# First operands of a recurrence made beside its decays' projections, loads in another order, squares ahead of weight sums, and products of ones on an idle TensorE

## The reference

```python
for i in range(2):                      # first block
    if i % 2 == 0:
        z = rmsnorm(h, mix_norm) @ mix_w_in          # 1024 x 3328
        y_a = rwkv7_bidir(z[..., :1792], ...)        # recurrence, both directions
        y_b = hyena_bidir(z[..., 1792:], ...)        # long convolution, filters made by a small MLP
        h = h + concat([y_a, y_b]) @ mix_w_out
    else:                                # neighbourhood attention
        ...
    h = h + conv_ffn(...); h = h + per_layer_embedding(...)

# rwkv7_bidir: r, k, v are neighbour-mixed slices of z
w  = exp(-exp(-softplus(-(w0 + tanh(wd) @ w_up)) - 0.5))   # decays
a  = sigmoid(a0 + ad @ a_up);  g = sigmoid(gd) @ g_up
kk = k * k_k / max(norm(k * k_k), 1e-12);  k = k * (1 + (a - 1) * k_a)
S  = S * w - (S kk) (kk a)^T + v k^T;  y = S r            # 256 steps

for l in range(2):                      # second block, 256 tokens and 256 of context
    x, ctx = half_ffn(...); x, ctx = token_mixing(...); x, ctx = half_ffn(...)
# half_ffn: h + 0.5 * gate * ((silu(n @ wg) * (n @ wu)) @ wd), n = modulate(rms_norm(h))
```

## Time and profile before

| | |
|---|---|
| median of 3 runs | 3163.56 us (3161.01 to 3167.01) |
| the profiled execution | 3160.99 us, its span 3159.5 us |
| mean granted TensorE clock | 0.985 |
| busy: PE, DVE, ACT, POOL | 95%, 44%, 18%, 1% |
| weights and tables read | 367.19 MB, mean 117 GB/s |

### The profile page before, as it was taken

How to read it: one execution, slowest core, us unless ns; L and a number is a source line. 1 busy time by engine, 2 the same in 40 slices (tenths; PEclk the granted TensorE clock), 3 DMA queues, 4 the chain that set the end, 5 groups by cost and what they waited for, 6 DMA issues and landing times.

```text
span 3159.5 us, 43436 instructions
## 1 busy us (share of the span) xinstructions
PE 2995.4 (95%) x18294; PEld 2415.3 (76%) x18294; DVE 1375.0 (44%) x2855; ACT 583.6 (18%) x1342; POOL 37.3 (1%) x60
## 2 busy tenths in 40 slices
PE   7978899999899989999999899999999999999999
PEld 5756678898488968888844447888878888765899
DVE  3265433533533534445222625445244453225675
ACT  1232222113312021000021621010010000224110
POOL 0000000002000000000000000000000000000000
PEclk9989999999999999999999999999999999999999
DMA  6668754356244442222212112222422322331353
GB/s 223 214 215 284 273 172 159 109 185 174 80 137 140 128 159 75 86 64 74 90 56 75 54 40 67 80 74 63 117 80 80 93 61 74 108 103 44 123 156 106
DMA packets 355844, 371.03 MB, mean 117 GB/s; under 512 B 7395, under 2 KB 282228, under 8 KB 355524
## 3 DMA queue, kind: packets, MB, share of 16 engines
q1 hardware_dynamic: 350224, 358.24, 36.0%
q0 software_dynamic: 2208, 5.31, 0.9%
q10 hardware_dynamic: 3220, 4.71, 0.4%
HBM read 367.19 MB, written 1.05 MB: 117 GB/s over the span
## 4 chain that ended last, share of the span: by engine, by line
PE 89%; DVE 6%; ACT 3%; issue 2%; DMA 1%; ACTq 0%; DVEq 0%
PE acc L132 73%; PE aux L132 15%; ACT sb_xn L267 1%; PE aux L2150 1%; DVE sb_work L1415 0%; DMA weights<-mix_w_in 0%; DVE sb_work L1886 0%; DVE sb_work L1883 0%; ACT sb_work L1685 0%; ACT sb_work L1687 0%; DMA sb_x<-xT 0%; DVE sb_work L1897 0%; ACT sb_rstd L258 0%; DVE sb_work L1665 0%; ACT sb_rstd L260 0%
## 5 line engine op out<-in xcount | busy, mean ns | idle before, releaser
L132 PE MATMUL acc<-sb_xn,weights 128*128 128x256 f32 (+2 forms) x5184 | 1220.1, 391 | 31.4 <-ACT sb_xn L267 17.6
L132 PEld LDWEIGHTS acc<-sb_xn,weights 128*128 128x128 f32 x5184 | 951.2, 192 | 257.3 <-issue 136.0
L132 PE MATMUL acc<-sb_work 128*128 128x256 f32 (+1 forms) x1936 | 373.1, 346 | 0.0
L132 PEld LDWEIGHTS acc<-sb_work 128*128 128x128 f32 x1936 | 323.0, 191 | 34.1
L132 PE MATMUL acc<-sb_work,weights 128*128 128x256 f32 (+2 forms) x1508 | 322.4, 361 | 3.2 <-DVE sb_work L1200 1.4
L132 PE MATMUL acc<-sb_big,weights 128*128 128x256 f32 (+1 forms) x1776 | 313.8, 333 | 4.1 <-issue 3.9
L132 PEld LDWEIGHTS acc<-sb_big,weights 128*128 128x128 f32 x1776 | 278.1, 191 | 30.8 <-issue 5.3
L132 PEld LDWEIGHTS acc<-sb_work,weights 128*128 128x128 f32 x1508 | 254.2, 191 | 54.3 <-issue 26.1
L1415 DVE TENSOR_TENSOR sb_work<-weights 128x512 f32<-128x512 f32 (+1 forms) x112 | 99.7, 890 | 160.5 <-PE acc L132 160.4
L1387 ACT COPY sb_work<-acc 128x256 f32<-128x256 f32 (+1 forms) x112 | 37.9, 339 | 704.2 <-PE acc L132 704.2
L132 PE MATMUL aux<-sb_xn,sb_work 128*128 128x256 f32 (+1 forms) x704 | 153.2, 362 | 6.5 <-ACT sb_xn L267 6.5
(11 more groups left out here) (304 smaller groups left out, 2553.0 us busy)
## 6 DMA issues: line engine op xcount, KB each, us to landing
weights<-ffn_w_up SPq DMA_DIRECT2D x88, 1024.0 KB, 7.9
weights<-w_mod SPq DMA_DIRECT2D x36, 2048.0 KB, 9.0
weights<-ffn_w_down SPq DMA_DIRECT2D x48, 1408.0 KB, 7.1
weights<-ffn_w_gate SPq DMA_DIRECT2D x44, 1024.0 KB, 5.5
weights<-w_in SPq DMA_DIRECT2D x8, 2048.0 KB, 8.0
weights<-mix_w_in SPq DMA_DIRECT2D x6, 2048.0 KB, 13.5
weights<-na_w_qkv SPq DMA_DIRECT2D x6, 2048.0 KB, 9.9
weights<-ple_w_gate SPq DMA_DIRECT2D x4, 2048.0 KB, 8.2
```

Source lines behind the costliest of these rows:

```text
L132: return te.matmul(o, lhsT, rhs, start=start, stop=stop, skip_group_check=True)
```

## The change

Six things are changed.

1. Loads: x is issued first on ACT's queue, then the four constants. The filter tables, the DFT matrices and the context move to SP's queue, between the blocks of `mix_w_in`. The masks' DMAs on POOL wait for x. The waits for the constants move behind the first norm's squares (DVE) and sums (PE); ACT's SiLU of the conditions moves behind the first norm.
2. PE gets products of ones with ones (`tensor_idle`), 128 x 128 each, whose result nobody reads: 22 at the program's start, 8 behind the first norm's sums, and 11 behind the sums of each of the six norms of the second block.
3. The four gate products go ahead of the projections, into two accumulator banks, and ACT copies them out with two wide copies ahead of the sigmoids.
4. For p = 0 the mixed key is made before DVE waits for the projections; ACT makes the key's copy and square between the sigmoids of n = 3 and n = 4, and PE sums the squares between n = 5 and n = 6. The temporaries get other places, and for p = 0 two of them are `dd` and `rho`. DVE's two modulation steps go behind the mixes.
5. ACT's first copy of the scan for p = 0 waits for the bonus sum.
6. In a half FFN DVE squares the odd tiles before the weight sums and scales, not behind them.

The core of the diff:

```diff
+    def tensor_idle(n):
+
+        for _ in range(n):
+            mm(aux[3][:, 0:128], ones[:], ones[:])
+
     def tensor_mix_in():
         tensor_norm(mix_norm)
+        tensor_idle(8)
+        te.wait_ge(const_in.sem, 64)
...
-    def scalar_lora(other):
+    def scalar_lora(other, first):
         ac.wait_ge(wad_set.sem, wad_set_at(1))
         wad_tanh.on(ac.activation(wad[0:64], wad[0:64], ACT.Tanh))
         other.to(14)
+        for b in range(2):
+            ac.wait_ge(gate.sem, gate_at(b))
+            gate_read.on(ac.copy(gg[:, 2 * b:2 * b + 2, :], area(acc[b], 0, 2, L)))
         for n in range(NG):
...
+            if n == 3:
+                next(first)
         other.to(MOD_EARLY)
-        for ct in range(CT):
-            ac.wait_ge(gate.sem, gate_at(ct))
-            gate_read.on(ac.copy(gg[:, ct, :], aux[ct][:, 0:L]))
...
+        for b in range(2):
+            te.wait_ge(acc_free[b].sem, scan_banks[b])
+            for ct in (2 * b, 2 * b + 1):
+                ins_ = mm(acc[b][:, L * (ct % 2):L * (ct % 2) + L], gup[:, 128 * ct:128 * ct + 128], gd2, ct % 2 == 0)
+            gate.on(ins_)
         te.wait_ge(wad_tanh.sem, wad_tanh_at(0))
         te.wait_ge(hy_out.sem, hy_out_at(3))
...
+            elif n == 5:
+                te.wait_ge(gate_read.sem, gate_read_at(1))
+                next(first)
+                next(first)
...
+        if p == 0:
+            shifted_mix(k_, 8)
         ve.wait_ge(lora_read.sem, lora_read_at(2 * p + 1))
...
     def tensor_half_ffn(F, following=None):
         tensor_norm(F.norm)
+        tensor_idle(11)
         tensor_fast(F.fast, F.norm.ready, following)
...
     def vector_half_ffn(F):
+        vector_squares(F.norm)
         sig, value = F.norm.x_ready[KT - 1]
         ve.wait_ge(sig.sem, value)
         vector_weight_sums(F.fast, 0, (0, 1, 2, 3))
         v_step.on(ve.tensor_scalar(half_gate, mod[:, F.m0 + 16:F.m0 + 24, :], 0.5, None, ALU.mult))
         vector_scales(F.l, 0 if F.j == 0 else 2, F.m0 + 8)
-        vector_norm(F.norm)
+        vector_scaled(F.norm)
...
     def tensor_mixing(M):
         tensor_norm(M.norm)
+        tensor_idle(11)
...
         sp.wait_ge(x_in.sem, 16)
-        sync_wide(mix_in, ins["mix_w_in"][0])
+        sync_wide(mix_in[0:1], ins["mix_w_in"][0])
+        for dst, src in ((feats[0:17], ins["c_feats"]), (fw[0:17, 0, :], ins["hy_f_w1"][0]), (fw[0:64, 1, :], ins["hy_f_w2"][0]),
+                         (fw[0:64, 2, :], ins["hy_f_w3"][0]), (w4[0:64], ins["hy_f_w4"][0]), (decay, ins["c_decay"])):
+            hy_in.on(sp.dma_start(dst, src))
+        sync_wide(mix_in[1:3], ins["mix_w_in"][0])
+        ctx_in.on(sp.dma_start(dft, ins["c_dft"]))
+        sync_wide(mix_in[3:4], ins["mix_w_in"][0])
+        ctx_in.on(sp.dma_start(x[:, :, 0:CTX], ins["ctxT"].rearrange("(k p) t -> p k t", p=128)))
+        sync_wide(mix_in[4:], ins["mix_w_in"][0])
...
+        x_in.on(ac.dma_start(x[:, :, CTX:T2], ins["xT"].rearrange("(k p) t -> p k t", p=128)))
+        for dst, src in ((col[:], ins["cols"]), (ident[:], ins["c_ident"]), (blk64[:], ins["c_blk64"]), (headm[:], ins["c_headm"])):
+            const_in.on(ac.dma_start(dst, src))
+        scalar_norm(mix_norm)
```

More of the change, by code:

```diff
@@ L703, in vector_prepare @@
             ve.wait_ge(sc_turn.sem, sc_turn_at(4 * p - 1))
-        shifted_mix(k_, 8)
+            shifted_mix(k_, 8)
+        else:
+            ve.wait_ge(gate.sem, gate_at(1))
         yield
@@ L736, in scalar_prepare, with key @@
     def scalar_prepare(p):
+        q, u = (t0, t1) if p else (dd, rho)
+        def key():
+            ac.wait_ge(pd_key.sem, pd_key_at(p))
+            ac.wait_ge(a_step.sem, a_step.n)
+            a_step.on(ac.activation(kk, k_, ACT.Copy, scale=cols("k_k", 1, p)))
+            pd_kksq.on(ac.activation(q, k_, ACT.Square, scale=cols("k_k", 1, p)))
+        if p == 0:
+            key()
+            yield
         ac.wait_ge(pd_cum.sem, pd_cum_at(p))
@@ L742, in scalar_prepare @@
         a_step.on(ac.activation(dd_next, t0, ACT.Exp, scale=-DECAY_C))
-        ac.wait_ge(pd_key.sem, pd_key_at(p))
-        ac.wait_ge(a_step.sem, a_step.n)
-        a_step.on(ac.activation(kk, k_, ACT.Copy, scale=cols("k_k", 1, p)))
-        pd_kksq.on(ac.activation(t0, k_, ACT.Square, scale=cols("k_k", 1, p)))
+        if p:
+            key()
         yield
@@ L749, in scalar_prepare @@
         ac.wait_ge(pd_clamp.sem, pd_clamp_at(p))
-        a_step.on(ac.activation(t1, t1, ACT.Ln))
+        a_step.on(ac.activation(u, u, ACT.Ln))
         ac.wait_ge(a_step.sem, a_step.n)
-        pd_unit.on(ac.activation(t1, t1, ACT.Exp, scale=-0.5))
+        pd_unit.on(ac.activation(u, u, ACT.Exp, scale=-0.5))
         yield
@@ L1093, in vector_scan, with tensor_recurrence @@
             (sc_out if par else v_step).on(ve.tensor_tensor(o, quads(aux[par][:, 0:256])[:, 2:4, :], o, ALU.add))
-    def tensor_recurrence(other):
-        te.wait_ge(gate_read.sem, gate_read_at(CT - 1))
-        for b in range(2):
-            te.wait_ge(acc_free[b].sem, scan_banks[b])
-        for _ in tensor_prepare(0):
+    def tensor_recurrence(other, first):
+        for _ in first:
             pass
@@ L1103, in tensor_recurrence, with scalar_recurrence @@
         other.to(MOD_STEPS)
-    def scalar_recurrence(other):
+    def scalar_recurrence(other, first):
         ac.preload_act_table_set(NAT_LOG)
-        for _ in scalar_prepare(0):
+        for _ in first:
             pass
@@ L1113, in vector_recurrence @@
     def vector_recurrence(other):
-        other.to(MOD_EARLY)
         vector_scan_setup()
-        for _ in vector_prepare(0):
-            pass
+        for n, _ in enumerate(vector_prepare(0)):
+            if n == 1:
+                other.to(MOD_EARLY)
         for p in range(NP):
@@ L2356, in tensor_program @@
         tensor_hyena(fill)
-        tensor_lora(fill)
-        tensor_recurrence(fill)
+        first = tensor_prepare(0)
+        tensor_lora(fill, first)
+        tensor_recurrence(fill, first)
         tensor_mix_out()
```

60 lines of the change are left out of this document (28 added, 32 removed).

## The result

| kernel | median us | lowest to highest | runs |
|---|---|---|---|
| before | 3165.3 | 3161.0 to 3170.1 | 4 |
| after | 3136.6 | 3131.6 to 3140.0 | 4 |

The ratio is 0.9908, 95% interval 0.9887 to 0.9929: 0.9% faster. The profiled execution took 3134.65 us with a span of 3133.4, against 3160.99 and 3159.5 before; the mean granted clock went from 0.985 to 0.991. The forecast of 3126 was 10.6 us too low; its range of 3117 to 3139 holds the time, near its upper end.

What follows compares the result with a forecast made beforehand. PE holds 89% of the chain, so time comes only where PE waits or runs at half clock. Terms 11.5 + 5.2 + 16.0 + 4.3 = 37.0 us off 3160.99, plus 2.6 to the median: forecast 3126, range 3117 to 3139.

Steps and rivals of the forecast that it cites:

- Sum of the start: Program start: earlier first weights 9.5, warm first group 2.3, less 0.3 for filter tables: gain 11.5 us (8 to 12.5).
- 8.2 us, landing at 14.2, say 14.4: Start: first weight block, constants and masks move at some 380 GB/s after x lands at 6; weights there at 14.4.
- 2.3 for a warm first group: Start: PE's first group takes 3.72 us at full clock instead of 6.05, a gain of 2.3 us.
- the loads hold the start: Rival, start: weights at 17 and tables 2 us late, or x later than 8; start gives 3 to 6; chance 0.11.
- Projections: Gate products first and key work between projections: recurrence's first product at 197.9 instead of 203.08, gain 5.2 us.
- Squares ahead: Half FFNs one, two and last: squares before weight sums let PE's sums end 5.1, 4.9, 5.9 earlier; 16.0 us (14 to 17).
- Eleven products: Products of ones behind six norms keep PE warm: 2.0 first mixing, 0.3 second, 2.0 half FFNs; 4.3 us (0 to 10).
- I take the fall as likely: Half FFNs: clock falls in the 2.8 us idle stretch before product 3, leaving 0.5 us gain for each of four.
- the modulation's weights take start and projections back: Rival, 131 to 400 us: modulation's weights are the true limit and cancel start and projections; 3143 us; chance 0.05.
- The clock holds in the half FFNs: Rival, half FFNs: PE is never idle for 3 us, so the clock stays; 5.9 us more, 3120 us; chance 0.14.
- Cold squares: Rival, half FFNs: PE is cold for the sums anyway, so squares give 10 instead of 16; 3133 us; chance 0.05.
- Less clock in dense stretches: Rival, long stretches: denser activity lowers the granted clock; at mean 0.960 about 3198 us, slower; chance 0.03.

Runs made afterwards that it cites:

- the start alone: Kernel before with only x first, the moved loads and waits, and the 22 and 8 products of ones around the first norm's sums: 3164.2 us against 3164.4.

## Why the prediction was right, and where its size was off

In the profiled span the change gained 26.1 us for a forecast of 37.0. The four terms came to about 35 at their places (8.3, 5.3 and 21.5, the last for squares and eleven products), and 9 were lost in stretches where I had nothing. The mechanisms of the first three terms are as forecast; the fourth comes out only in its sum. That the range holds the time is in part luck: no end of it was set for such a loss. Its upper gain is also mis-added (the four ends give 46.1, not 46.5), which would move the range by half a microsecond.

**Sum of the start (11.5): 8.3 in place, inside its ends of 8 to 12.5.** The step that failed is "8.2 us, landing at 14.2, say 14.4". The block was issued at 6.8 and used at 16.3: x landed 0.8 us later than the 6 that I took, and the block took 9.5 us instead of 8.2. In these 9.5 us the queues moved 3.05 MB, as much as the sum has, but at 321 GB/s and not at the 380 of the earlier trace rows; only 0.28 MB of it were constants and 0.38 MB were what stands behind the block on SP's queue. Why the rate was lower is open. The table load behind x's wait (1.28 us) was not foreseen either; it is hidden, since the norm is ready at 13.8. With weights late, PE stood 2.2 us instead of 0.6 and the "2.3 for a warm first group" became 0.7 in this execution. The rival "the loads hold the start" came near for the weights (16.3, its 17), but the filter's tables were on time and the start gave more than its 3 to 6.

**Projections (5.2): right,** 5.3 in the trace and 4.9 by itself; each step of the working stands within 0.3 us.

**Squares ahead (16.0): the mechanism is right, the size too low.** The sums end at 1170.7 in the kernel with this edit alone, as worked out, and up to product 3 the three places give 15.4. In the whole span it gives 18.0, and by the medians 21.0 (18.0 to 25.6), above my end of 17: what the clock does behind product 3 was not in the term.

**Eleven products (4.3): right in sum, not in its parts.** 5.2 by the medians, not clear of noise, and 3.5 by the rows: the first mixing gives 3.0 for 2.0, the half FFNs 0.1 for 2.0. "I take the fall as likely" was borne out at two of four, the first and the third; behind the other two's 2.6 and 1.2 us of idle time the clock held. The Trainium skill, page "TensorE: Matmul & The Clock Gate", section "Why this matters for your kernels", warns only of gaps above some 3 us. The traces agree at some rows and not at others: the clock fell behind 1.95 and 2.76 us and held behind 1.96 and 2.77.

**What the sum left out: 9 us lost in stretches that the change does not touch.** 4.5 at the long convolution, which no term or rival had, though the idle stretch of 2.76 us stood in the trace of before, with the clock held. And 4.0 in the recurrence. The step behind it is the argument on the rival that the modulation's weights take start and projections back: "SP waits for PE: the ring is full and weights wait for products, so an earlier PE is not starved". It is true of weights and was taken for the whole. What PE lacks are its own instructions, whose packets come late behind the weights' bursts: with half the modulation's bytes most of these waits are gone. In the kernel with the start alone, waits and the falls of the clock behind them took back all 8.3 us.

**The other rivals.** Modulation takes it back: right in effect for the start alone (the weights themselves were not late, the instructions were), 4 of 14 us in the whole change. The clock holds in the half FFNs: in two of four. Cold squares: no. Less clock in dense stretches: the mean rose to 0.991, so it falls.

## What to carry to other kernels

A part that starts earlier keeps its lead only if every stretch behind it takes as long as before: read the lead at several common rows, not at the end. Where many short instructions run beside heavy loads, look for waits on the fullest engine that name no releaser, and count instructions between them; until there is less traffic in that stretch, a shorter start can be worth nothing (here 0.2 us with all of the loads and 10.7 with half of them). Judge changes of 0.3% by medians of many executions, since executions of one kernel lie up to 15 us apart, and falls of the clock that one trace has are missing in the next.

## What the hardware showed that I had not expected

- PE stops for 0.5 to 2.8 us within a row of equal products, 126.4 passes or a multiple of it apart, 1.2 to 1.6 us after a 16 KB packet of the queue "instruction" and right after bursts of 285 to 418 GB/s; with 144 instead of 271 GB/s in the stretch five such waits became one.
- The same idle stretch (2.76 and 2.77 us, the same program ahead of it) cost the clock in one execution and not in another. Also behind the wait of 1.95 us at 607 us in the kernel after the clock fell, and behind one of 1.96 at the same place before it held. What decides it these runs leave open.
- Behind the first norm's sums a pass of one column took 0.11 us, like one of 128 columns: 44 of the one and 16 of the other take 6.75 us.
- ScalarE's first table load began only when the wait of the activation behind it was over (6.86 us, x's landing); asked for ahead of the wait it began at 3.54.
